# Two-block transformer forward on one core: first attention units and their normalizations reordered, GpSimd's bias in pieces, and the first two output tiles of a gated projection computed together

## The chip, the cores and the metric

One Trainium2 chip, one of its NeuronCores. The metric is the device time of one execution in microseconds, the median of several runs. TensorE is called PE here, its weight loads PEld, VectorE DVE, ScalarE ACT, GpSimd POOL, and SyncE, which only issues weight transfers, SP.

## What is computed

Two blocks in a row, each of two layers, on 256 tokens of width 1024 (the first block puts 16 extra tokens in front, so its tiles are 272 tokens wide). All matrices are float32. Two pieces matter for the change.

The first layer is an attention with eight heads in which each query attends to its 64 best keys only:

```python
q, k, v, qi, ki, wi = jnp.split(h @ w_in, A_SPLITS, axis=-1)
score = jnp.einsum('bqh,bqhs->bqs', wib, jax.nn.relu(s))      # s = qi . ki
_, idx = lax.top_k(score, k_top)
logits = jnp.einsum('bqgrd,bqkgd->bqgrk', qg, ksel) * scale + bias
p = jax.nn.softmax(logits, axis=-1)
o = jnp.einsum('bqgrk,bqkgd->bqgrd', p, vsel)
```

The first layer of the second block is a gated mixer:

```python
z = jax.nn.gelu(hn @ w_in, approximate=False)
u, v = jnp.split(z, 2, axis=-1)
v = layernorm(v, ln_g, ln_b)
sv = jnp.einsum('gij,bnjgc->bnigc', ws, vb) + b_s.T[None, None, :, :, None]
return (u * sv.reshape(B, S, GATE_DIM)) @ w_out
```

## The kernel before

Everything is held transposed, with the model's width on the partitions and tokens in the free dimension. The program is a list of stages (`STAGES`); in each, PE makes output tiles of 128 rows from 128x1024 blocks of weights. SP loads a block into one of four slots of `w_raw`; ACT writes its rounded part to `w_hi`, DVE the rest to `w_lo` (function `prep`, always three blocks ahead), and PE makes the product from two or three passes with them (`mm2`, `mm3`). A block's slot is free for the next when PE has counted `block_done`. Output tiles rotate through four PSUM banks, `stream`; `misc` are the other four. Each engine runs its own instructions strictly in order, and semaphores join the engines; the order of the work is written out by hand for each engine.

**First attention (stage "in", then `attention(att_a, ...)`).** There are 16 units (a head and a block of queries), eight of block A with 144 keys, then eight of block B with 272. For unit u, PE makes `logits` (L721, and L727 which adds the mask `keep` of the chosen keys), DVE adds the bias and takes the maximum (`score_a`, L2502), ACT takes the exponential (L1474), DVE multiplies by the inverse sum (`softmax_norm`: L2209, L2218), PE transposes (`turn_probs`, L749), ACT copies (L1484), and PE multiplies with the values (`outputs`, L762). Logits go alternately to `misc[0]` and `stream[2]`. On PE, `logits(0)` is followed by `after_first` (sums of squares of the last head, L711), `meta_logits` (the 16 extra tokens, L796) and `keep_warm(stream[2], 16)`, 16 products whose result nobody reads (L734). Then come `logits(1)` and the loop of the units: in turn u, `logits(u + 2)`, `turn_probs(u)`, `outputs(u - 1)`.

The choice of the 64 keys is a generator on DVE, `selection` (L2360, L2361: eight maxima and their replacement; L2364 writes the mask). It is advanced two steps in each of the last turns of stage "in" and for its last two steps at unit 0 in `rest_of_selection`, together with `query_sums` (L2384), on which POOL waits. POOL then computes factors (L1964, L1967) and four blocks of bias, `masked_bias` (L1979): block A, heads 0 to 3; block B, heads 0 to 3; then the same for heads 4 to 7 (`half == 1`). A unit's score waits for its block of bias.

**Gated mixer (stages "gv", "gu", "gout").** "gv" makes the v half, DVE normalizes it (L2701). "gu" makes 16 tiles of the u half; after tile g, PE does `spatial(g - 1)` (L1214), four small products into `misc[c % 2]`, which for c of 2 and more waits until DVE has read the result of c - 2 (`sv_read`, given by L2721). DVE turns it into a product (`gated(c)`: L2718, L2721, L2728), ACT rounds it (L1773), and POOL makes the low part (L2054), which counts `gp_lo`. "gout" multiplies with `w_out`: eight output tiles of two weight blocks each, 16 steps k of two passes (L619, L620), and step k of the first tile waits for `gp_lo` at k + 1. DVE adds each tile to `h` (L2140, L2143) and writes the low part of the next input (L2153, `low`); in this stage DVE runs a hardware loop of two turns of four tiles, PE four tiles written out and then one turn.

Of the kernel before, what the change touches and what calls it, by code (L numbers as in the profile page):

```python
# [20 lines left out]
ALU = mybir.AluOpType  # L21
# [3 lines left out]
P = 128  # L25
D = 1024
DT = D // P
META = 16
# [10 lines left out]
GT = GATE // P  # L39
# [6 lines left out]
R = 4  # L46
LR = 3
# [40 lines left out]
ST = {s.name: s for s in STAGES}  # L88
# [64 lines left out]
def build(nc, x, meta, table, w_in_a, w_o_a, w_kv_b, w_q_b, w_o_b, w_up, w_down, a_w_in, a_w_s,  # L153
          a_b_s, a_w_out, b_w_q_a, b_w_q_b, b_w_o, kv_w_a, kv_w_b, mlp_w1, mlp_w2, positions,
          vecs, lams, consts, onehot, out):
    with ExitStack() as ctx:
# [11 lines left out]
        wide_h, wide_l = split_w[:, 0, :], split_w[:, 1, :]  # L168
# [8 lines left out]
        ones = sb("ones", [P, P])  # L177
# [426 lines left out]
        def _(pe):  # L604
# [126 lines left out]
            def keep_warm(dst, n):  # L731

                for _ in range(n):
                    pe.matmul(dst[:, 0:T], xh[:, 0, 0:P], xh[:, 1, :], start=True, stop=True)  # L734
# [30 lines left out]
            def attention(att, q_of, v_of, after_first=None):  # L765
                n = len(att.units)
                own_meta = att.name != "c"
                logits(att, q_of, 0)
                if own_meta:
                    after_first()  # L770
                    meta_logits(att, q_of)
                    keep_warm(stream[2], 16)
                logits(att, q_of, 1)
                for u in range(n + 1):
                    if u + 2 < n:
                        logits(att, q_of, u + 2)
                    if u < n:
                        turn_probs(att, u)
                    if u == 8 and own_meta:
                        meta_turn(att)  # L780
                    if u == 11 and own_meta:
                        meta_outputs(att, v_of)
                    if u >= 1:
                        v = u - 1
                        if v >= 4 and v % 2 == 0:
                            pe.wait_ge(att.oh, att.ob + v // 2 - 1)
                            pe.wait_ge(att.ol, att.ob + v // 2 - 1)
                        outputs(att, v_of, v, PV_BANK[v // 2 % 2][:, P * (v % 2):P * (v % 2 + 1)])
# [133 lines left out]
            def up(name, t0, first=None):  # L922
# [31 lines left out]
                        product(s, i, g, **src)  # L954
                sweep(pe, s, group, peel=True)

            def down(name, t0, nk, stride, sem_, base):
                s = ST[name]

                def ready(k):  # L960
                    pe.wait_ge(sem_, base + k + 1)
                skip = stride - (T - t0)
                hid = lambda buf: lambda k: buf[:, k * stride + skip:(k + 1) * stride]
                both = None
                if name in HALVES:
                    both = lambda k: split_w[:, :, k * stride + skip:(k + 1) * stride]
                sweep(pe, s, lambda s, i, g: product(s, i, g, hid(wide_h), hid(wide_l), t0,
                                                     ready, nk, both), peel=True)

            simple("wo_a", lambda s: from_heads(att_a))  # L970
            up("up0", 0, CONV_IN[0])
# [247 lines left out]
            pe.wait_ge(S["tile_read"], s.t0)  # L1219
            for g in range(16):  # L1220
                product(s, None, g, **from_x(s, META))
                if g >= 1:
                    spatial(g - 1)
            spatial(15)
            down("gout", META, GT, 256, gp_lo, 0)
            up("mlp0", META)
            down("mlpd0", META, F2T, 256, mlp["lo"], 0)
# [666 lines left out]
        def _(pool):  # L1894
# [75 lines left out]
            def masked_bias(qt, half):  # L1970

                q, hi = TT[qt], TOK[qt][1]
                o = P if qt == "A" else 0
                dst = bias_a[qt][:, 4 * half:4 * half + 4, :]
                g = fq_a[:, 12 * half + q:12 * half + q + 10:3].unsqueeze(2)
                pool.wait_ge(roots_ready, 1 if half == 0 else 2 if qt == "A" else 3)
                pool.wait_ge(S["skew_loaded"], SKEW_IN)
                pool.wait_ge(skew_masked, 1)
                pool.tensor_tensor(dst, sk[:, 4 * half:4 * half + 4, o:o + hi],  # L1979
                                   g.to_broadcast([P, 4, hi]), ALU.mult).then_inc(bias_ready, 1)  # L1980

            pair_half = neg_half[:, 0:12].rearrange("p (m x) -> p m x", m=2)

# [88 lines left out]
        def _(dve):  # L2072
# [62 lines left out]
            def residual_stage(name, t0, straight=False, beside={}):  # L2135
# [23 lines left out]
                def group(s, i, g):  # L2159
                    for b in range(s.bpg - 1):  # L2160
                        prep(s, i, g * s.bpg + b)
                    add(s, i, g)
                    between = s.bpg == 1 and g % 4 != 3
                    if between:
                        prep(s, i, g)
                    low(s, i, g)
                    if not between:
                        prep(s, i, (g + 1) * s.bpg - 1)
                    if g in beside:
                        beside[g]()  # L2170
# [41 lines left out]
            def softmax_norm(att, v):  # L2212

                hh, qt = att.units[v]
                lo, hi = att.keys(qt)
                k = inverse_sums(att, v)
                p0 = lg[:, v % LR, 0, lo:hi]
                dve.tensor_scalar(p0, p0, ri[:, k:k + 1], None, ALU.mult).then_inc(att.p, 1)  # L2218

            def softmax_mix(att, v):  # L2220

# [262 lines left out]
            def rest_of_selection(u):  # L2484

                if u == 0:
                    dve.wait_ge(a_ssq, 10)
                    query_sums(att_a, 1)
                if u < 7:
                    next(selection, None)  # L2490
                if u == 0:
                    next(selection, None)
                if u == 16:
                    dve.wait_ge(att_a.mo0, att_a.meta + 1)
# [244 lines left out]
            stage("gu", gu_after)  # L2739
            gated(14)  # L2740
            gated(15)
            residual_stage("gout", META)

            def angles():

# [256 lines left out]
```

## Time and profile before

| | us |
|---|---|
| median of 3 runs | 1305.34 (1304.49 to 1305.48) |
| the profiled execution, its own time | 1305.53 |
| its span, first to last instruction | 1303.7 |
| around the span | 1.8 |
| PE busy | 1281.2 (98%) |
| DVE busy | 979.8 (75%) |
| ACT busy | 669.0 (51%) |
| POOL busy | 493.8 (38%) |
| mean granted clock of TensorE | 0.998 |

Busy times of PE are modelled ends of pipelined products, so that neighbours overlap; the start of a product against the start of the one before it tells more than its length. A number in square brackets behind a row of the timeline is the idle time of that engine just before the instruction, with the instruction that ended it.

### The profile page before, as it was taken

To read this page: it belongs to the slowest core of one execution; us is meant where nothing else is said; L and a number is where in the kernel's file an instruction comes from. 1 tells how busy PE (TensorE), PEld (TensorE's weight loads), DVE (VectorE), ACT (ScalarE), POOL (GpSimd) and SP (SyncE) were. 2 spreads that over 40 slices of the span, in tenths; PEclk is the share of its full clock that TensorE was granted. 3 is DMA by queue.
4 is the path that set the end of the run, shared out by engine and by line. 5 is a ranking of instruction groups with operands and counts; after the bars stand their busy time and mean duration, and the time that the engine had idled before them with its cause. 6 is when DMAs were issued, how large, how long until landed. Compare 5 with 4: busy or idle time off the path is not lost.

```text
span 1303.7 us, 26999 instructions
## 1 busy us (share of the span) xinstructions
PE 1281.2 (98%) x8914; PEld 1182.5 (91%) x8914; DVE 979.8 (75%) x1564; ACT 669.0 (51%) x1103; POOL 493.8 (38%) x454
## 2 busy tenths in 40 slices
PE   8999999999999999999999999999999999999998
PEld 7999999999999989999888898888888987888887
DVE  5686899975666668999765687799866866999553
ACT  5445555554455555666545455355444565455442
POOL 1042455541212216555311032299611001799222
PEclk9999999999999999999999999999999999999999
DMA  8631556566633316666567565666666642666762
GB/s 219 154 98 50 160 167 185 167 176 175 181 103 109 98 37 176 181 188 188 168 198 225 147 177 161 184 182 190 188 193 194 150 134 78 181 190 190 205 190 81
DMA packets 403204, 209.20 MB, mean 160 GB/s; under 512 B 20553, under 2 KB 397681, under 8 KB 403105
## 3 DMA queue, kind: packets, MB, share of 16 engines
q1 hardware_dynamic: 402016, 205.37, 55.0%
q0 software_dynamic: 784, 2.51, 0.8%
q8 instruction: 52, 0.85, 0.3%
q10 hardware_dynamic: 320, 0.21, 0.1%
q14 instruction: 32, 0.25, 0.1%
HBM read 206.98 MB, written 1.27 MB: 160 GB/s over the span
## 4 chain that ended last, share of the span: by engine, by line
PE 90%; DVE 6%; issue 2%; POOL 1%; ACT 1%; DMA 0%; DVEq 0%; POOLq 0%; ACTq 0%
PE bank L619 22%; PE bank L613 14%; PE bank L614 14%; PE bank L615 14%; PE bank L620 12%; DVE w_lo L2081 2%; PE bank L762 2%; PE bank L721 1%; PE bank L749 1%; PE bank L1184 1%; PE bank L1186 1%; PE bank L1185 1%; PE bank L1036 1%; PE bank L1023 1%; PE bank L691 1%
## 5 line engine op out<-in xcount | busy, mean ns | idle before, releaser
L2081 DVE TENSOR_TENSOR w_lo<-w_raw,w_hi 128x1024 fp32r<-128x1024 f32 x391 | 514.3, 1328 | 29.3 <-ACT w_hi L1441 28.4
L1441 ACT ACTIVATE w_hi<-w_raw 128x1024 fp32r<-128x1024 f32 x391 | 410.6, 1053 | 128.5 <-PE bank L620 66.0
L613 PE MATMUL bank<-split_x,w_lo 128*128 128x272 f32 (+2 forms) x1128 | 328.9, 292 | 0.2 <-issue 0.2
L615 PE MATMUL bank<-split_x,w_hi 128*128 128x272 f32 (+2 forms) x1128 | 322.5, 286 | 0.0
L614 PE MATMUL bank<-split_x,w_hi 128*128 128x272 f32 (+2 forms) x1128 | 322.4, 286 | 0.0
L619 PE MATMUL bank<-split_w,w_hi 128*128 128x512 f32 x880 | 307.7, 393 | 0.7 <-POOL split_w L1940 0.5
L620 PE MATMUL bank<-split_w,w_lo 128*128 128x256 f32 x880 | 246.6, 280 | 0.0
L613 PEld LDWEIGHTS bank<-split_x,w_lo 128*128 128x128 f32 x1128 | 212.2, 188 | 2.8 <-issue 0.6
L614 PEld LDWEIGHTS bank<-split_x,w_hi 128*128 128x128 f32 x1128 | 212.2, 188 | 0.3
L615 PEld LDWEIGHTS bank<-split_x,w_hi 128*128 128x128 f32 x1128 | 212.2, 188 | 0.3
L619 PEld LDWEIGHTS bank<-split_w,w_hi 128*128 128x128 f32 x880 | 164.9, 187 | 38.4 <-POOL split_w L1940 0.8
L619 PE MATMUL bank<-split_x,w_hi 128*128 128x512 f32 x512 | 179.5, 394 | 0.7 <-DVE split_x L2153 0.7
L620 PEld LDWEIGHTS bank<-split_w,w_lo 128*128 128x128 f32 x880 | 166.1, 189 | 0.0
L1915 POOL TENSOR_TENSOR sq_t<-h 128x256 f32<-128x256 f32 (+1 forms) x55 | 54.1, 984 | 250.6 <-DVE h L2143 250.1
L620 PE MATMUL bank<-split_x,w_lo 128*128 128x256 f32 x512 | 143.6, 281 | 0.0
L613 PE MATMUL bank<-split_w,w_lo 128*128 128x272 f32 (+1 forms) x444 | 130.5, 294 | 0.1
L615 PE MATMUL bank<-split_w,w_hi 128*128 128x272 f32 (+1 forms) x444 | 127.9, 288 | 0.0
L614 PE MATMUL bank<-split_w,w_hi 128*128 128x272 f32 (+1 forms) x444 | 127.4, 287 | 0.0
L619 PEld LDWEIGHTS bank<-split_x,w_hi 128*128 128x128 f32 x512 | 96.1, 188 | 22.7 <-DVE split_x L2153 1.0
L2529 DVE SCALAR_TENSOR_TENSOR scr<-scr,vec 128x256 f32<-128x256 f32 (+2 forms) x176 | 103.9, 600 | 12.7 <-ACT scr L1728 0.9
L1934 POOL TENSOR_TENSOR scr<-scr 128x272 f32<-128x272 f32 (+1 forms) x44 | 67.3, 1530 | 106.9 <-ACT scr L1735 85.0
L1728 ACT ACTIVATE scr<-scr,vec 128x272 f32<-128x272 f32 (+1 forms) x88 | 53.5, 608 | 101.0 <-DVE scr L2517 99.9
(295 smaller groups left out, 1855.9 us busy)
## 6 DMA issues: line engine op xcount, KB each, us to landing
w_raw<-in_mlp_w_dram SPq DMA_DIRECT2D x256, 256.0 KB, 3.2
w_raw<-in_w_up_dram SPq DMA_DIRECT2D x176, 256.0 KB, 3.3
w_raw<-in_w_down_dram SPq DMA_DIRECT2D x64, 256.0 KB, 3.4
w_raw<-in_a_w_in_dram SPq DMA_DIRECT2D x64, 256.0 KB, 3.5
w_raw<-in_w_in_a_dram SPq DMA_DIRECT2D x32, 256.0 KB, 4.1
w_raw<-in_w_kv_b_dram SPq DMA_DIRECT2D x32, 256.0 KB, 3.2
w_raw<-in_a_w_out_dram SPq DMA_DIRECT2D x32, 256.0 KB, 3.3
w_raw<-in_w_down_dram SPq DMA_DIRECT2D x32, 192.0 KB, 4.2
```

The costliest lines, as they stand in the source:

```text
L613: pe.matmul(dst, lo, mov_h, start=first, stop=False)
L614: pe.matmul(dst, hi, mov_l, start=False, stop=False)
L615: return pe.matmul(dst, hi, mov_h, start=False, stop=last)
L619: pe.matmul(dst.rearrange("p (s t) -> p s t", s=2), hi, both, start=first, stop=False)
L620: return pe.matmul(dst[:, 0:256], lo, mov_h, start=False, stop=last)
L762: ins = pe.matmul(dst, a, c, start=x_ == 0, stop=x_ == len(bls) - 1)
L1441: act.activation(w_hi[:, n % R, :], w_raw[:, n % R, :], ACT.Copy)\
L1728: act.activation(c_ring[:, g, c0:T], u_ring[:, g, c0:T], ACT.Identity, scale=vcol("conv_w", i, 4, o + 2 * UPT + g), bias=vcol("conv_b", i, ...
L1915: done(pool, pool.tensor_tensor(sq_t[:, t0:T], h[:, m, t0:T], h[:, m, t0:T], ALU.mult), "pool")
L1934: pool.tensor_tensor(gated, gated, c_ring[:, 2 * p, c0:T], ALU.mult)\
L2081: dve.tensor_tensor(w_lo[:, n % R, :], w_raw[:, n % R, :], w_hi[:, n % R, :].bitcast(F32), ALU.subtract)\
L2529: dve.scalar_tensor_tensor(c_, u_ring[:, q, lo - back:T - back], vcol("conv_w", i, 4, o + (CONV - 1 - back) * UPT + q), c_, ALU.mult, ALU. ...
```

## The change

In the first attention, PE makes `logits(1)` right behind `logits(0)`, with a wait for the reading of stage "in"'s tile 15 (it was the last to use `stream[3]`, and tile 14 the last to use `stream[2]`). The unread products go to `stream[3]` and are six in place of 16. DVE's last two steps of `selection` move from unit 0 to units 2 and 3. For units 0 to 5 DVE normalizes with an operation of three operands (the probabilities, the inverse sum, and a column of ones broadcast) in place of `tensor_scalar`. POOL computes both blocks of bias of heads 4 to 7 head by head, so eight operations in place of two.

In the gated mixer, `spatial(0)` moves behind tile 2 of "gu", directly ahead of `spatial(1)`. `spatial(15)` moves from ahead of "gout" to its first output tile, ahead of step k = 4. Output tiles 0 and 1 of "gout" are made in turns, in the new function `two_outputs`: steps 0 to 7 of tile 0, steps 0 to 7 of tile 1, steps 8 to 15 of tile 0, steps 8 to 15 of tile 1; the slot of tile 1's first block is counted free only with its second. DVE prepares both of the first tile's two blocks ahead of adding the tile, and its eight tiles are written out without a hardware loop.

```diff
                 logits(att, q_of, 0)
                 if own_meta:
+                    pe.wait_ge(S["tile_read"], ST["in"].t0 + 16)
+                    logits(att, q_of, 1)
                     after_first()
                     meta_logits(att, q_of)
-                    keep_warm(stream[2], 16)
-                logits(att, q_of, 1)
+                    keep_warm(stream[3], 6)
+                else:
+                    logits(att, q_of, 1)
...
+            def two_outputs(s, dst_of, mov_h, both, ready):
+
+                for g in range(2):
+                    bank_free(s, None, g)
+                for b in range(2):
+                    for g in range(2):
+                        j = 2 * g + b
+                        slot = (s.n0 + j) % R
+                        pe.wait_ge(S["lo_ready"], s.n0 + j + 1)
+                        for k in range(8 * b, 8 * b + 8):
+                            if g == 0 and k == 4:
+                                spatial(15)
+                            if g == 0:
+                                ready(k)
+                            w = slice((k - 8 * b) * P, (k - 8 * b + 1) * P)
+                            ins = mm2(dst_of(g), w_lo[:, slot, w], w_hi[:, slot, w], mov_h(k),
+                                      both(k), k == 0, k == GT - 1)
+                        if j != 2:
+                            ins.then_inc(S["block_done"], 2 if j == 3 else 1)
...
-                sweep(pe, s, lambda s, i, g: product(s, i, g, hid(wide_h), hid(wide_l), t0,
-                                                     ready, nk, both), peel=True)
+                def group(s, i, g):
+                    if name != "gout" or i is not None or g >= 2:
+                        product(s, i, g, hid(wide_h), hid(wide_l), t0, ready, nk, both)
+                    elif g == 0:
+                        two_outputs(s, lambda g: stream[(s.t0 + g) % R][:, :], hid(wide_h), both,
+                                    ready)
+                sweep(pe, s, group, peel=True)
...
                 product(s, None, g, **from_x(s, META))
-                if g >= 1:
+                if g == 2:
+                    spatial(0)
+                if g >= 2:
                     spatial(g - 1)
-            spatial(15)
             down("gout", META, GT, 256, gp_lo, 0)
...
-                pool.tensor_tensor(dst, sk[:, 4 * half:4 * half + 4, o:o + hi],
-                                   g.to_broadcast([P, 4, hi]), ALU.mult).then_inc(bias_ready, 1)
+                for hs in [slice(0, 4)] if half == 0 else [slice(e, e + 1) for e in range(4)]:
+                    ins = pool.tensor_tensor(dst[:, hs, :], sk[:, 4 * half:4 * half + 4, o:o + hi][:, hs, :],
+                                             g[:, hs, :].to_broadcast([P, hs.stop - hs.start, hi]),
+                                             ALU.mult)
+                ins.then_inc(bias_ready, 1)
...
+                    joined = s.name == "gout" and i is None and g == 0
+                    if joined:
+                        prep(s, i, g * s.bpg + 1)
                     add(s, i, g)
...
-                    if not between:
+                    if not between and not joined:
                         prep(s, i, (g + 1) * s.bpg - 1)
...
-                p0 = lg[:, v % LR, 0, lo:hi]
-                dve.tensor_scalar(p0, p0, ri[:, k:k + 1], None, ALU.mult).then_inc(att.p, 1)
+                probs = lg[:, v % LR, 0, lo:hi]
+                if att.name == "a" and v < 6:
+                    dve.scalar_tensor_tensor(probs, probs, ri[:, k:k + 1],
+                                             ones[:, 0:1].to_broadcast([P, hi - lo]), ALU.mult,
+                                             ALU.mult).then_inc(att.p, 1)
+                    return
+                dve.tensor_scalar(probs, probs, ri[:, k:k + 1], None, ALU.mult).then_inc(att.p, 1)
...
-                if u < 7:
-                    next(selection, None)
-                if u == 0:
+                if 2 <= u < 8:
                     next(selection, None)
...
-            residual_stage("gout", META)
+            residual_stage("gout", META, straight=True)
```

## Rows read from the trace of the kernel before

**Rows 1.** The page: busy time of each engine.

```profile
PE 1281.2 (98%) x8914; PEld 1182.5 (91%) x8914; DVE 979.8 (75%) x1564; ACT 669.0 (51%) x1103; POOL 493.8 (38%) x454
```

**Rows 2.** Chain that ended last, start of the attention: start us, us, what.

```profile
84.40 0.61 PE bank L711 x6
...
85.73 2.22 PE bank L734 x16
87.95 0.24 PE bank L721 x2
...
90.62 1.50 DVE scr L2218
...
92.16 0.44 PE bank L749 x2
```

**Rows 3.** Timeline of DVE and POOL in units 0 to 3.

```profile
84.67 0.37 DVE L2502 CUSTOM_DVE_ANT_0 scr<-bank,vbuf,small 128x144 f32<-128x144 f32 x1
...
85.44 0.43 DVE L2360 MAX8 small<-qk 128x8 f32<-128x272 f32 x1
...
86.45 0.30 DVE L2364 TENSOR_SCALAR split_w<-qk 128x272 fp32r<-128x272 f32 x1
...
86.89 1.15 POOL L1979 TENSOR_TENSOR vbuf<-skew,small 128x576 f32<-128x576 f32 x1
...
88.30 0.37 DVE L2502 CUSTOM_DVE_ANT_0 scr<-bank,vbuf,small 128x144 f32<-128x144 f32 x1 [1.54 <-PE bank L727]
...
88.78 0.30 DVE L2218 TENSOR_SCALAR scr<-scr,small 128x144 f32<-128x144 f32 x1
...
90.00 2.01 POOL L1979 TENSOR_TENSOR vbuf<-skew,small 128x1088 f32<-128x1088 f32 x1
...
90.62 1.48 DVE L2218 TENSOR_SCALAR scr<-scr,small 128x144 f32<-128x144 f32 x1
```

**Rows 4.** The same timeline earlier, where DVE and POOL meet.

```profile
77.20 1.96 DVE L2081 TENSOR_TENSOR w_lo<-w_raw,w_hi 128x1024 fp32r<-128x1024 f32 x1
78.04 2.99 POOL L1979 TENSOR_TENSOR vbuf<-skew,small 128x1088 f32<-128x1088 f32 x1
```

**Rows 5.** Line L2718 alone: duration ns min/median/max.

```profile
L2718 DVE SCALAR_TENSOR_TENSOR scr<-qk,vec x16: 341/344/830, 749.9 to 796.1; 128x128 f32<-128x128 f32 x16
```

**Rows 6.** Timeline at the start of "gu".

```profile
744.43 0.28 PE L614 MATMUL bank<-split_x,w_hi 128*128 128x256 f32 x1
744.54 0.28 PE L615 MATMUL bank<-split_x,w_hi 128*128 128x256 f32 x1
745.34 0.71 PE L1214 MATMUL bank<-qk,vbuf 128*128 128x128 f32 x4 [0.52 <-DVE vbuf L2701]
...
746.86 1.22 DVE L2081 TENSOR_TENSOR w_lo<-w_raw,w_hi 128x1024 fp32r<-128x1024 f32 x1
```

**Rows 7.** Timeline from "gu" to "gout".

```profile
792.92 0.71 PE L1214 MATMUL bank<-qk,vbuf 128*128 128x128 f32 x4 [0.85 <-DVE scr L2721]
...
797.98 0.40 PE L619 MATMUL bank<-split_w,w_hi 128*128 128x512 f32 x1
...
798.27 0.74 POOL L2054 TENSOR_TENSOR split_w<-scr,split_w 128x256 fp32r<-128x256 f32 x1 [0.81 <-ACT split_w L1773]
798.33 0.39 PE L619 MATMUL bank<-split_w,w_hi 128*128 128x512 f32 x1
...
799.06 0.50 PE L619 MATMUL bank<-split_w,w_hi 128*128 128x512 f32 x1 [0.23 <-POOL split_w L2054]
799.17 1.23 DVE L2081 TENSOR_TENSOR w_lo<-w_raw,w_hi 128x1024 fp32r<-128x1024 f32 x1 [1.43 <-ACT w_hi L1441]
```

**Rows 8.** Windows: us, busy PE, PEld, DVE, ACT, POOL, clock, DMA.

```profile
88.00:92.00 4.00, 2.55 (x20) 2.04 (x18) 3.33 (x12) 1.98 (x8) 3.84 (x4) 1.00 0.01 2
...
464.00:466.00 2.00, 1.24 (x10) 0.76 (x7) 1.86 (x6) 1.28 (x7) 0.68 (x1) 1.00 0.00 0
...
472.00:474.00 2.00, 2.00 (x11) 1.92 (x11) 0.03 (x1) 0.63 (x3) 0.00 (x0) 0.50 0.00 0
```

## The prediction

> **What bounds the kernel now.** I read the page first: PE is busy in 98% of the span, DVE in 75% [rows 1], and the chain of work that ended last runs on PE but for short pieces. Time is gained only where PE waits, so I looked up the idle times on PE at the places of the edits. There are three. In the first attention's start PE waits for normalized probabilities: the chain leaves PE for DVE's L2218 at 90.62 and comes back at 92.16 [rows 2]. At the start of "gu", `spatial(0)` waits for the layer normalization [rows 6]. Between "gu" and "gout", `spatial(15)` waits 0.85 us for DVE's reading of c = 13, and step 15 of the first tile waits for POOL's last low part [rows 7]. Everything behind each place runs off PE in the same order, so what PE wins there moves the end by as much, unless a new wait takes it back.
>
> **Attention, the order.** The reader is to see in [rows 3] that DVE does score 0 at 84.67, its sums and two selection steps until 86.75, and then idles 1.54 us until 88.30, for `logits(1)`. These start at 87.95 only, behind 2.22 us of unread products [rows 2]. The new order, step by step:
> - `logits(1)` starts at 84.40; DVE has it 0.35 later (87.95 to 88.30), at 84.75.
> - PE's sums of squares come 0.33 later (a unit's two products), end at 84.40 + 0.33 + 0.61 = 85.34. The meta logits took 85.73 - 85.01 = 0.72, and six unread products take 6 x 2.22/16 = 0.83: PE is at `logits(2)` at 86.89 and at `turn_probs(0)` at 87.2.
> - DVE: query sums from 85.34, 0.43 (85.01 to 85.44) to score 1 at 85.77; a score's start to its normalization's is 0.48 (88.30 to 88.78); so unit 0 is normalized from 86.25, ready at 86.6. PE doesn't wait at all.
> - Score 2 at 86.89 + 0.35 = 87.24, normalization 1 from 87.72, which meets POOL (below) and ends by 88.3. One selection step is 1.01 (85.44 to 86.45): score 3 at 89.2, normalization 2 from 89.7, ready at 90.05. `turn_probs(2)` starts at 90.1 in place of 92.16: 2.1 us earlier. The last selection step, 0.30, lies behind it and not ahead of it. The mask of block B is due at unit 8.
>
> **Attention, the three operands and the pieces.** The `tensor_scalar` of unit 2 took 1.48 in place of 0.30 and ended 0.09 behind POOL's bias of 2.01 [rows 3]: it was held until POOL was through. An operation with two tensors in SBUF is no better off by this trace. L2718 takes 0.344 and 0.830 at most, where it met POOL [rows 5]; L2081 began at 77.20, POOL's next operation at 78.04, and they took 1.96 and 2.99 against 1.22 and 2.01 alone [rows 3, 4, 6]: POOL ran up to 78.04, DVE got in between POOL's two operations, and the second then stood behind DVE. So whoever started first keeps the other out, and DVE gets its turn at the end of a POOL operation. The new form (probabilities and ones both in SBUF) still waits; the pieces shorten the wait. From 576 elements in 1.15 and 1088 in 2.01 an operation costs 0.18 plus 1.68 ns an element: a piece of block A is 0.42, of block B 0.64, and a block as a whole 0.54 longer. The Trainium skill has this as a rule (SBUF — State Buffer, Who interferes with whom): a Vector instruction with two SBUF inputs contends with a GpSimd instruction that reads SBUF, and the loser is blocked until the other is done. By that rule the three operands gain nothing here, the trace agrees (0.830 against 0.344), and were it wrong the sum would lack the collision term below.
>
> The new form was not run at this size; its nearest row is the score of 144 columns with two tensors, 0.37, against 0.30: 0.07 dearer, six times 0.4, of which only units on DVE's path count; above nothing and below 0.4, included in the times above.
> Bias A of heads 4 to 7 starts 0.33 later and takes 0.54 more, so it is ready at 86.89 + 0.33 + 1.15 + 0.54 = 88.9, at most 0.4 more for one DVE operation in between; unit 4's score comes at about 90.2. POOL's block B started 1.96 behind A's end, so now at about 91.1, and lasts until 94 to 94.5. Due at unit 12, it holds nobody; but the normalizations of units 4, 5 and 6 fall into it, each held from 0 to 0.64. PE's own work per unit hides part. I take 0.4 for the three (about the mean of 0.32 each, less half hidden); the bounds are 0 and 3 x 0.64 = 1.9. **Attention: 2.1 - 0.4 = 1.7 us gained, from 0.2 to 2.1.**
>
> **Start of "gu".** The last product of tile 1 starts at 744.54, its follower would start 0.12 later (744.43 to 744.54), at 744.66, and `spatial(0)` starts at 745.34 [rows 6]: 0.68 lost. Behind tile 2 (24 products, 24 x 0.118 = 2.8 us later) it finds its input. Does the new order run into the next thing? PE wants tile 3's weights at 744.66 + 2.83 + 2 x 0.45 = 748.4; they are ready at 746.86 + 1.22 = 748.08 [rows 6]. A margin of 0.3. **0.7 us gained, from 0.3 to 0.7.**
>
> **"gu" to "gout".** Before, PE stood 0.85 for `spatial(15)`. Now it does steps 0 to 3 of tile 0 meanwhile (four times 0.35, 797.98 to 798.33, makes 1.4 us), and comes to it after DVE's release. Step 15 of the first tile started at 799.06, where 798.33 + 0.35 = 798.68 was due: 0.38 lost [rows 7]. In the new order eight steps of tile 1 (2.8 us) stand ahead of it: due at about 800.7, POOL's part is there at 799.01. Taken off: 1.23; added, one more change between the two kinds of products, 0.1 (0 to 0.2). What could be late next are weights. Tile 1's second block is wanted at about 801.1 and ready at 799.17 + 1.23 = 800.4: margin 0.7. Tile 2's first (DVE's second preparation, now directly behind) at 801.6, wanted at 804. Tile 2's second needs only a slot that is free at 801.1. Tile 3's first needs the slot freed at 804; behind ACT's part and DVE's queue (adding tile 1, its low part, then 1.2 for the block) I estimate it at 808.6 for 809.6. These hold by 0.7 to 2.4. The DVE loop written out removes a loop step that is beside PE's work: nothing, and if its cover were gone 0.1. **1.1 us gained, from 0.4 (a late block) to 1.3.**
>
> **Sum.** 1.7 + 0.7 + 1.1 = 3.5 us. The profiled execution took 1305.53, 1.8 around its span of 1303.7, and stands 0.2 above the median; its time would be 1302.0, the median 1305.34 - 3.5 = 1301.8.
>
> **Rivals.**
> - Collisions decide. If each normalization of units 1 to 6 waits out a whole piece or more, the attention gains 0.2 to 0.8. For it: DVE holds [rows 3, 5], and more POOL operations give more chances to meet. Against: DVE gets in at the end of one [rows 4]. 0.5 + 0.7 + 1.1 = 2.3: 1303.0.
> - The clock falls in the attention, which has 1.4 us fewer unread products. It fell elsewhere: at 472 the granted clock was 0.50, 1.2 GHz in place of 2.4, after a stretch like 464 to 466, where PE was busy 1.24 of 2 us; from 88 to 92, 2.55 of 4, it stayed [rows 8]. In the new order PE waits less in that very stretch. A fall of some 3.4 us costs half, 1.7: 1303.5.
> - The joined tiles run into late weights and give back what they won, 1.1: 1302.9. Decides at the margins of 0.7 and 1.0 above.
> - The reordering doesn't do it: unit 0 or 1 waits on something else (the sums, the exponential), and only "gu" and "gout" win: 1303.5.
> - Slower: the clock stays down for all of the attention. From 87 to 99 at the lower level costs up to 6 us, against 3.5 won: 1307.8. It becomes slower from 7 us at the lower level on. Against it: PE is busier there than before, and before it kept its clock.
>
> **Chances.** My forecast 0.66, its own range 1300.9 to 1302.7 (the terms' likely ends); collisions 0.13; the falling clock 0.06; late weights 0.06; no effect in the attention 0.06; slower 0.03. The measurement tells 0.2%, 2.6 us, from no change. The forecast lies on the faster side nearly always (0.64), collisions and late weights in four of ten cases between them (0.07), the rest within: faster 0.71, same 0.26, slower 0.03. The range reaches to the collisions and the fall, 1300.8 to 1303.7.
>
> **What would show it.** L2502 of unit 1 without an idle time and some 2.5 us earlier; L749 of unit 2 about 2.1 us earlier; no L2218-like operation above 1 us, but the new ones of units 1, 4 and 5 above 0.4; no idle time ahead of the first L1214; none ahead of the last L1214 and of step 15; the granted clock 1.00 from 84 to 100. The prediction is wrong if PE's idle times come back as waits for `w_lo` in "gout", if unit 4 or 5 waits for its bias, or if the clock falls.

## The result and the profile after

The changed kernel took **1303.07 us** in the median of 20 runs (1300.08 to 1306.12), the kernel before 1305.34 in 20 runs beside it (1303.26 to 1307.72): the medians are 2.3 us apart. The recorded ratio is 0.9985, interval 0.9978 to 0.9991, which makes 1.2 to 2.9 us gained. The median is inside the range of 1300.8 to 1303.7, 1.3 above the forecast of 1301.8 and above the forecast's own range (1300.9 to 1302.7). It lies within 0.2% (2.6 us) of no change, where the prediction had put only 0.26 of its chances, against 0.71 for more than that.

The profiled execution of the changed kernel took 1300.44, with a span of 1298.6: 5.1 below the profiled execution of before, far more than the 2.3 of the medians. The page's first part of the changed kernel:

```profile
PE 1276.5 (98%) x8904; PEld 1178.4 (91%) x8904; DVE 981.2 (76%) x1564; ACT 669.3 (52%) x1103; POOL 496.7 (38%) x460
```

PE has ten products fewer (the unread ones) and POOL six operations more. To lay the two traces side by side I took the starts of DVE's blocks `w_lo` (the same 394 in every kernel, on L2081 before and L2114 after), whose pace is PE's. Three intervals hold nearly all of the difference: A from the block ahead of the first attention to the one behind it, B the last 31 us of the second attention, C from the first tiles of "gu" to the stage behind "gout".

| kernel, profiled execution | A | B | C |
|---|---|---|---|
| before | 37.14 | 30.70 | 94.88 |
| before again (e1) | 37.15 | 30.69 | 94.08 |
| changed | 35.67 | 29.59 | 92.01 |
| changed again (e2) | 35.66 | 32.27 | 91.95 |
| changed, a third time (e10) | 35.66 | 32.22 | 92.51 |

A, from such rows (timeline of DVE, kernel before, then the changed kernel; start us, us, what): 118.64 - 81.50 = 37.14, and 117.24 - 81.57 = 35.67.

```profile
81.50 1.23 DVE L2081 TENSOR_TENSOR w_lo<-w_raw,w_hi 128x1024 fp32r<-128x1024 f32 x1 [0.43 <-ACT w_hi L1441]
...
118.64 1.22 DVE L2081 TENSOR_TENSOR w_lo<-w_raw,w_hi 128x1024 fp32r<-128x1024 f32 x1
```

```profile
81.57 1.23 DVE L2114 TENSOR_TENSOR w_lo<-w_raw,w_hi 128x1024 fp32r<-128x1024 f32 x1 [0.43 <-ACT w_hi L1471]
...
117.24 1.22 DVE L2114 TENSOR_TENSOR w_lo<-w_raw,w_hi 128x1024 fp32r<-128x1024 f32 x1
```

A is the same to 0.01 in every execution of a kernel. B is not, and C has a part of 0.5 to 0.8 that comes and goes. The change touches nothing in B. The stretch ahead of A varies too: from the first block `w_lo` to the one at A's start it is 71.15 in the kernel before and 71.85 in e1, and 0.5 to 1.0 longer than 71.15 in five of the 14 profiles (e1, e2, e9, e10, e12), whichever the kernel.

**The attention after**, timelines of PE, DVE and POOL of the changed kernel, against [rows 2 to 4]; the whole trace is 0.08 later here than before:

```profile
86.94 0.41 PE L721 MATMUL bank<-qk 128*128 128x144 f32 x2
...
87.26 0.39 PE L749 MATMUL bank<-cst,scr 128*128 128x128 f32 x2
...
88.63 0.44 PE L749 MATMUL bank<-cst,scr 128*128 128x128 f32 x2 [0.68 <-DVE scr L2255]
...
90.42 0.44 PE L749 MATMUL bank<-cst,scr 128*128 128x128 f32 x2 [0.58 <-DVE scr L2255]
...
91.84 0.44 PE L749 MATMUL bank<-cst,scr 128*128 128x128 f32 x2 [0.23 <-DVE scr L2255]
```

```profile
85.87 0.36 DVE L2541 CUSTOM_DVE_ANT_0 scr<-bank,vbuf,small 128x144 f32<-128x144 f32 x1
...
86.35 0.37 DVE L2255 SCALAR_TENSOR_TENSOR scr<-scr,small,ones 128x144 f32<-128x144 f32 x1
87.46 0.37 DVE L2541 CUSTOM_DVE_ANT_0 scr<-bank,vbuf,small 128x144 f32<-128x144 f32 x1 [0.74 <-PE bank L727]
...
87.94 0.63 DVE L2255 SCALAR_TENSOR_TENSOR scr<-scr,small,ones 128x144 f32<-128x144 f32 x1
...
90.97 0.82 DVE L2255 SCALAR_TENSOR_TENSOR scr<-scr,small,ones 128x144 f32<-128x144 f32 x1
```

```profile
87.22 1.65 POOL L2010 TENSOR_TENSOR vbuf<-skew,small 128x144 f32<-128x144 f32 x4
...
90.98 2.67 POOL L2010 TENSOR_TENSOR vbuf<-skew,small 128x272 f32<-128x272 f32 x4
```

The reader is to see that `turn_probs(2)` starts at 90.42 where it was 92.16, that the two long normalizations (0.63 and 0.82, the others 0.37) meet POOL's pieces of bias (87.94 lies inside the row from 87.22; the row at 90.97 starts 0.01 ahead of POOL's at 90.98 and was held all the same), and that nothing is held as long as the 1.48 of before.

**"gu" and "gout" after**, timelines of PE and DVE, against [rows 6, 7]:

```profile
744.88 0.28 PE L615 MATMUL bank<-split_x,w_hi 128*128 128x256 f32 x1
745.00 1.05 PE L1243 MATMUL bank<-qk,vbuf 128*128 128x128 f32 x8
...
788.17 0.61 PE L1243 MATMUL bank<-qk,vbuf 128*128 128x128 f32 x4
788.54 0.47 PE L619 MATMUL bank<-split_w,w_hi 128*128 128x512 f32 x1
...
789.89 0.28 PE L620 MATMUL bank<-split_w,w_lo 128*128 128x256 f32 x1
790.01 0.60 PE L1243 MATMUL bank<-qk,vbuf 128*128 128x128 f32 x4
790.37 0.48 PE L619 MATMUL bank<-split_w,w_hi 128*128 128x512 f32 x1
...
805.37 0.39 PE L619 MATMUL bank<-split_w,w_hi 128*128 128x512 f32 x1
...
805.90 0.47 PE L619 MATMUL bank<-split_w,w_hi 128*128 128x512 f32 x1
```

```profile
803.58 1.08 DVE L2186 SCALAR_TENSOR_TENSOR split_x<-h,vec,split_x 128x272 fp32r<-128x272 f32 x1 [0.79 <-ACT split_x L1488]
804.59 2.34 DVE L2114 TENSOR_TENSOR w_lo<-w_raw,w_hi 128x1024 fp32r<-128x1024 f32 x2
```

`spatial(0)` and `spatial(1)` (one row of eight products at 745.00) and `spatial(15)` (790.01) start 0.12 behind the product ahead of them: no wait. One new loss is there: a step of 805.90 - 805.37 = 0.53 where 0.35 is usual, as the first block of tile 3 came late. DVE's low part ahead of it took 1.08 (0.50 four us earlier), beside an operation of POOL (803.62 to 804.36).

### The profile page after: what moved, and what is told of

Read it like the earlier page. It is cut to its first block, busy times and chain, and to the rows that moved or that the text cites. A ratio compares the mean times of both kernels' runs of the same rounds, so it can differ in the third digit from the quotient of the medians.

```text
span 1298.6 us, 26922 instructions
## 1 busy us (share of the span) xinstructions
PE 1276.5 (98%) x8904; PEld 1178.4 (91%) x8904; DVE 981.2 (76%) x1564; ACT 669.3 (52%) x1103; POOL 496.7 (38%) x460
## 4 chain that ended last, share of the span: by engine, by line
PE 90%; DVE 6%; issue 1%; POOL 1%; ACT 1%; DMA 0%; DVEq 0%; POOLq 0%; ACTq 0%
PE bank L619 23%; PE bank L613 15%; PE bank L615 14%; PE bank L614 14%; PE bank L620 12%; DVE w_lo L2114 1%; PE bank L762 1%; PE bank L721 1%; PE bank L1213 1%; PE bank L1215 1%; PE bank L1214 1%; PE bank L749 1%; PE bank L1065 1%; PE bank L1052 1%; PE bank L1243 1%
## 5 line engine op out<-in xcount | busy, mean ns | idle before, releaser
L2114 DVE TENSOR_TENSOR w_lo<-w_raw,w_hi 128x1024 fp32r<-128x1024 f32 x391 | 517.8, 1337 | 29.9 <-ACT w_hi L1471 28.9
```

The lines of the kernel that those rows point to most:

```text
L2114: dve.tensor_tensor(w_lo[:, n % R, :], w_raw[:, n % R, :], w_hi[:, n % R, :].bitcast(F32), ALU.subtract)\
```

## The experiments

Each was timed beside the kernel before, whose median was 1305.17 for e1 to e4, 1305.33 for e5 to e8 and 1305.34 for e9 to e12.

### e1 and e2: both kernels again

The kernel before and the changed one, nothing altered.

> The kernel before, unchanged, for its spread and for the granted clock of each of its runs. Theory 1 (the changed kernel gains 1.5 in the attention, 0.8 at the start of gu and 1.1 between gu and gout, and the clock falls as often as before): its runs' clocks spread like those of the changed kernel, from 0.994 to 0.998, and at one clock it is 3.4 us or more slower. Theory 2 (fewer unread products let the clock fall more often in the changed kernel, which takes back some 2 us of the median): its clocks lie higher, at 0.997 to 0.998 in most runs, and the time stays at 1305.3.

> The changed kernel, unchanged, beside the kernel before on one chip. Both theories: ratio 0.9975 to 0.999. Theory 2: again clocks of 0.994 to 0.998 with the time 1.3 us longer for each 0.001, and more than one level among its runs. The profile is wanted for the step time of gout: 0.347 us in the first profile of the changed kernel, 0.353 in the one of before. If it belongs to the kernel's order it is 0.347 again and 0.353 in the run of before; if it is chance, it varies.

e1: 1305.14, ratio 1.0 (0.999 to 1.0009). e2: 1303.22, ratio 0.998 (0.997 to 0.9991). So the gain of about 2 stands, and the 5.1 of the profiled execution doesn't: e2's own profile has B at 32.27 in place of 29.59. The windows of both profiles there, first the changed kernel's, then e2's (stretch, length, busy PE, PEld, DVE, ACT, POOL, granted clock, DMA):

```profile
464.00:466.00 2.00, 0.99 (x14) 0.95 (x15) 1.90 (x7) 1.27 (x5) 0.00 (x0) 1.00 0.00 0
466.00:468.00 2.00, 2.00 (x19) 1.85 (x18) 1.90 (x7) 1.92 (x8) 0.02 (x1) 1.00 0.00 0
...
472.00:474.00 2.00, 1.78 (x13) 1.59 (x14) 1.31 (x5) 1.43 (x5) 0.28 (x1) 1.00 0.00 0
```

```profile
466.00:468.00 2.00, 2.00 (x11) 2.00 (x10) 1.93 (x7) 1.68 (x8) 0.00 (x0) 0.50 0.00 0
468.00:470.00 2.00, 2.00 (x15) 1.75 (x14) 1.12 (x5) 1.07 (x5) 0.70 (x1) 0.76 0.00 0
470.00:472.00 2.00, 2.00 (x16) 1.69 (x16) 0.53 (x4) 1.18 (x4) 0.30 (x1) 1.00 0.00 0
472.00:474.00 2.00, 2.00 (x13) 1.83 (x13) 0.44 (x1) 0.93 (x4) 0.25 (x1) 0.60 0.00 0
474.00:476.00 2.00, 2.00 (x12) 2.00 (x11) 0.64 (x2) 0.45 (x2) 0.00 (x0) 0.55 0.00 0
```

The granted clock is the column of 1.00, 0.50 and so on. It stayed at 2.4 GHz through this stretch in one execution of the changed kernel and fell to 1.2 GHz twice in another; in the kernel before it fell once [rows 8]. B reads 29.59 without a fall (changed, e6, e12), 30.68 to 30.70 with one (before, e1, e3, e4, e5, e7, e8), 32.09 to 32.27 with two (e2, e10, e11): 1.1 us for one, 2.5 to 2.7 for two.

### e3, e4 and e8: the parts alone

e3 is the kernel before with all of the change's edits in the attention; e4 the kernel before with all of those in the gated mixer; e8 the kernel before with `spatial(0)` moved alone. The core of each, in this order:

```diff
+                    logits(att, q_of, 1)
                     after_first()
                     meta_logits(att, q_of)
-                    keep_warm(stream[2], 16)
+                    keep_warm(stream[3], 6)
```

```diff
+                    elif g == 0:
+                        two_outputs(s, lambda g: stream[(s.t0 + g) % R][:, :], hid(wide_h), both,
+                                    ready)
...
-            spatial(15)
             down("gout", META, GT, 256, gp_lo, 0)
```

```diff
                 product(s, None, g, **from_x(s, META))
-                if g >= 1:
+                if g == 2:
+                    spatial(0)
+                if g >= 2:
                     spatial(g - 1)
```

> The kernel before with the attention's edits alone. Theory 1: 1.5 us faster, ratio 0.9989. Theory 2: the clock falls more often, and the ratio is 1.000 or above, with clocks of 0.994 to 0.997 in many runs.

> The kernel before with the edits of gu and gout alone. Theory 1: 1.9 us faster, up to 2.7 if the faster steps of gout belong to the order: ratio 0.9980 to 0.9986. Theory 2: the same, and clocks as for the kernel before, so that this part alone gives more than the whole change.

> The kernel before with spatial(0) behind tile 2 and nothing else. The first wait, 0.68 to 0.78 us, goes: 1304.5, ratio 0.9994. Its profile is also one more look at gout in the old order: steps of 0.347 or 0.353 us, and whether they change at the stall ahead of step 15 of tile 0. If the step time belongs to the order, it is 0.353 behind the stall; in a new look at the kernel before it was 0.347, so it should be either.

| | us, median | ratio | A | B | C |
|---|---|---|---|---|---|
| e3, attention | 1304.37 | 0.9993 (0.9984 to 1.0002) | 35.66 | 30.68 | 94.89 |
| e4, mixer | 1303.02 | 0.9987 (0.9978 to 0.9996) | 37.14 | 30.69 | 92.00 |
| e8, `spatial(0)` | 1304.41 | 0.9994 (0.9985 to 1.0003) | 37.15 | 30.70 | 93.34 |

In the traces each part gives what it gives in the whole: the attention 37.14 - 35.66 = 1.48, `spatial(0)` 94.08 - 93.34 = 0.74 against e1, and the joined tiles 93.34 - 92.00 = 1.34. Their sum is 3.56. In the medians the mixer gives 2.15 and the attention only 0.8; e3's interval reaches from 2.1 faster to 0.3 slower, so it holds the 1.48 as well. e4 doesn't tell the joined tiles, the move of `spatial(15)` and the written-out DVE loop apart; no run has one of them alone.

### e5: 16 unread products again

The changed kernel, with 16 unread products in the first attention in place of 6.

```diff
-                    keep_warm(stream[3], 6)
+                    keep_warm(stream[3], 16)
```

> The changed kernel with 16 unread products in stream[3] in place of six. Theory 1 (the falls of the clock have nothing to do with the attention): logits(2) stands 10 x 0.139 = 1.4 us later behind them, so this is up to 1.0 us slower than the changed kernel, 1304.0, with mean clocks of 0.996 as before. Theory 2 (fewer unread products let the clock fall): the clocks go back to 0.998 in most runs as in the kernel before, and the time is 1302 to 1303, faster than the changed kernel or level with it.

1303.16, ratio 0.9982 (0.9974 to 0.9991). A is 36.87: only 0.27 below the kernel before, and 1.20 above the changed kernel. Yet the median is no higher than that of the changed kernel (1303.07, 1303.22 and 1303.13 in its three sets of runs): what ten products cost in A doesn't show in it, and e11 below takes that up.

### e6: the three operands undone

The changed kernel with `tensor_scalar` for the normalizations again.

```diff
-                if att.name == "a" and v < 6:
-                    dve.scalar_tensor_tensor(probs, probs, ri[:, k:k + 1],
-                                             ones[:, 0:1].to_broadcast([P, hi - lo]), ALU.mult,
-                                             ALU.mult).then_inc(att.p, 1)
-                    return
```

> The changed kernel with tensor_scalar for units 0 to 5 again. By the rows of before an operation with two tensors in SBUF is held as well as this one: no change beyond 0.4 us (0.07 less for each of six), 1303.1. In the profile L2218's successor takes 0.30 where it is free and 0.5 to 0.8 where it meets a piece of the bias. The rival, that the three operands escape POOL: normalizations above 0.8 us appear, and the time is 0.5 us or more longer.

1302.97, ratio 0.9984 (0.9972 to 0.9995); A is 35.65, against 35.67 and 35.66. The three-operand form wins nothing. Its cheapest row is 0.37 where `tensor_scalar` takes 0.30; the longest are alike. By form, L2255 of the changed kernel and then L2254 of e6, in the first units (busy us, mean ns | idle before):

```profile
L2255 DVE SCALAR_TENSOR_TENSOR scr<-scr,small,ones 128x144 f32<-128x144 f32 x6 | 2.9, 488 | 0.2
```

```profile
L2254 DVE TENSOR_SCALAR scr<-scr,small 128x144 f32<-128x144 f32 x8 | 3.5, 442 | 0.3
```

### e7: the bias in whole blocks again

The changed kernel with two operations in place of the eight.

```diff
-                for hs in [slice(0, 4)] if half == 0 else [slice(e, e + 1) for e in range(4)]:
-                    ins = pool.tensor_tensor(dst[:, hs, :], sk[:, 4 * half:4 * half + 4, o:o + hi][:, hs, :],
...
+                pool.tensor_tensor(dst, sk[:, 4 * half:4 * half + 4, o:o + hi],
+                                   g.to_broadcast([P, 4, hi]), ALU.mult).then_inc(bias_ready, 1)
```

> The changed kernel with the two blocks of bias of heads 4 to 7 as one operation each. If the lock goes by operations, unit 1's normalization is held until block A is through (some 1.1 us in place of 0.63) and unit 3's or 4's until block B is through (1.5 to 2.0), so the attention wins 0.5 to 1.5 us less: 1303.7 to 1304.6. If the pieces have no effect: 1303.1 and the same chain.

1303.31, ratio 0.9987 (0.9978 to 0.9996). The median can't tell; A can: 36.52, so the pieces are worth 0.85 us. The rows are plain (e7, timelines of DVE, POOL and PE):

```profile
90.61 1.70 DVE L2252 SCALAR_TENSOR_TENSOR scr<-scr,small,ones 128x144 f32<-128x144 f32 x1
```

```profile
90.14 2.01 POOL L2009 TENSOR_TENSOR vbuf<-skew,small 128x1088 f32<-128x1088 f32 x1
```

```profile
92.36 0.44 PE L749 MATMUL bank<-cst,scr 128*128 128x128 f32 x2 [1.11 <-DVE scr L2252]
```

Unit 3's normalization began at 90.61, inside POOL's one long operation (90.14 to 92.15), was held to its end, and PE waited 1.11 for it. With pieces the same normalization took 0.82 and PE waited 0.23.

### e10 and e11: what ten unread products do in both attentions

e10 is the changed kernel a third time. e11 is the kernel before with one line altered:

```diff
-                    keep_warm(stream[2], 16)
+                    keep_warm(stream[2], 6)
```

> The changed kernel again, beside the other three on one chip. 1303.2, with clocks of 0.996 or lower in about half of its runs (32 of 55 so far among it and the two variants with six unread products and both parts of the change).

> The kernel before with six in place of 16 unread products in the first attention, nothing else. DVE waits for logits(1), which come 1.4 us earlier: score 1 at 86.9 in place of 88.3. Theory 1: unit 0 is ready 1.4 us earlier; POOL's block B of the bias stays where it is, at 90.0 to 92.0, and holds unit 2's or a later unit's normalization less, so 0.5 to 1.4 us faster, clocks as before (none at 0.996). Theory 2, that fewer unread products in the first attention make the falls: clocks of 0.996 and lower in half of the runs, and no gain in the median.

e10: 1303.13, ratio 0.998 (0.9971 to 0.9989). e11: 1305.61, ratio 0.9997 (0.9988 to 1.0006), although A is 36.05. So six unread products alone, in the old order, win 1.09 in A, and it doesn't show in the median. Where it went can be read in e11's profile, B = 32.09, two falls (windows):

```profile
466.00:468.00 2.00, 2.00 (x10) 2.00 (x11) 1.97 (x5) 1.53 (x8) 0.00 (x0) 0.50 0.00 0
468.00:470.00 2.00, 2.00 (x16) 1.75 (x14) 1.33 (x7) 1.36 (x5) 0.70 (x1) 0.80 0.00 0
470.00:472.00 2.00, 2.00 (x17) 1.69 (x17) 0.47 (x3) 1.18 (x4) 0.23 (x1) 1.00 0.00 0
472.00:474.00 2.00, 2.00 (x13) 1.92 (x12) 0.50 (x1) 0.66 (x3) 0.32 (x1) 0.56 0.00 0
```

Every run gives its mean granted clock. In the profiles 0.997 to 0.999 stands for one fall or none in B, 0.996 for two, 0.994 for one of 10 us (e9). The mean isn't a clean count of falls in B, since every profile has one more at its end, behind PE's last product, which costs PE nothing but takes 0.001 to 0.002 off the mean. For runs without a profile the falls are inferred from this number. I counted the runs at 0.996 or below, with the mean time in each group:

| kernel | unread products, first attention | runs at 0.996 or below | mean us there | mean us at 0.998 |
|---|---|---|---|---|
| before | 16 | 7 of 96 | 1308.48 | 1305.15 |
| e1, e4, e5, e8 | 16 | 6 of 45 | | |
| e11 | 6 | 6 of 11 | 1306.21 | 1304.01 |
| changed, first 20 runs | 6 | 13 of 20 | 1304.17 | 1301.40 |
| e2, e10 | 6 | 13 of 22 | | 1301.60 (e10) |
| e6, e7 | 6 | 13 of 24 | | 1301.35 (e6) |
| e3 | 6 | 1 of 11 | 1307.50 | 1303.37 |

At a mean clock of 0.998 (which holds runs with one fall and some without) the changed kernel is 1305.15 - 1301.40 = 3.75 us faster, about the sum of the terms. That rests on four runs, from 1300.08 to 1302.78; e2 against the kernel before on its own chip gives the same, 1305.46 - 1301.68 = 3.8 at 0.997 and 1304.13 - 1300.28 = 3.9 at 0.999 (three and two runs of e2). The changed kernel's median is only 2.3 lower because more than half of its runs have, by their mean clock, a second or a long fall, and where a profile shows one it lies in the second attention, 370 us behind the edit. Six in place of 16 unread products in the first attention go with it: e11 differs from the kernel before by nothing else, on the same chip, and had 6 of 11 such runs against 2 of 28; and e5, the changed kernel with 16, had 1 of 11. What became frequent is a mean of 0.996, in the profiles two falls: 33 of 88 runs with six, 2 of 141 with 16. At 0.995 or below there are 13 of 88 and 11 of 141. e3 speaks against the simple form of that: it has six as well, and only 1 of 11.

### e9 and e12: unread products in the second attention

In both, PE makes six more unread products in the last units of the second attention, where it otherwise waits 0.86 us for DVE. The longer wait of 1.06 just behind stays as it was (timelines of PE, the changed kernel and then e9):

```profile
462.35 0.52 PE L1013 MATMUL bank<-cst,acc 128*128 128x128 f32 x3 [0.86 <-DVE split_w L2640]
...
465.01 0.35 PE L810 MATMUL bank<-cst,sq_t 16*16 16x16 f32 x8 [1.06 <-DVE sq_t L2345]
```

```profile
463.03 0.52 PE L1013 MATMUL bank<-cst,acc 128*128 128x128 f32 x3
...
465.70 0.36 PE L810 MATMUL bank<-cst,sq_t 16*16 16x16 f32 x8 [1.07 <-DVE sq_t L2346]
```

The six cost the path nothing there: between these two rows lie 2.66 us in the changed kernel and 2.67 in e9, and `logits_b(15)` ahead of them starts 1.95 and 1.94 before the first.

```diff
             turn_probs(att_b, 12)
             logits_b(15)
+            keep_warm(stream[3], 6)
```

e9 is the changed kernel with that; e12 has 16 unread products in the first attention as well:

```diff
-                    keep_warm(stream[3], 6)
+                    keep_warm(stream[3], 16)
```

> The changed kernel with six more unread products in the second attention's last units, behind logits_b(15), where PE idles 0.9 us. In all ten profiles so far the clock fell only there, between 465 and 473 us, once or twice or not at all. If the falls there spread the changed kernel's runs (1300 to 1306), the granted clock rises to 0.998 or 0.999 in most runs, and the median comes to 1301.5 (4 us below the kernel before). If unread products have no hold on the falls: clocks of 0.994 to 0.998 as for the changed kernel, 1303.2.

> The changed kernel with 16 unread products in the first attention and six more in the second. Theory 1: 0.5 to 1.0 us slower than with six and six, the work of the unread products in the first attention, 1302.3. Theory 2: fewer falls than with six and six, and level with it or faster.

| | us, median | runs | ratio | runs at 0.996 or below |
|---|---|---|---|---|
| e9 | 1301.40 (1300.80 to 1305.21) | 6 | 0.9967 (0.9954 to 0.9979) | 1 of 6 |
| e12 | 1302.42 (1301.56 to 1302.99) | 11 | 0.9978 (0.9969 to 0.9987) | 0 of 11 |
| e10, beside them | 1303.13 (1300.07 to 1305.98) | 11 | 0.998 (0.9971 to 0.9989) | 7 of 11 |

e12 has no run at 0.996 or below and a spread of 1.4 us where e10 has 5.9; it pays with A = 36.87. What its six products in the second attention add to that isn't shown, as e5, without them, had only 1 of 11. e9 keeps A = 35.66 and gives the lowest median, 3.9 below the kernel before, as much as the whole sum of the terms. Its one profiled run is the one with the long fall (B = 33.85):

```profile
466.00:468.00 2.00, 2.00 (x13) 2.00 (x11) 1.93 (x5) 1.55 (x8) 0.00 (x0) 0.59 0.00 0
468.00:470.00 2.00, 2.00 (x10) 1.75 (x9) 1.56 (x7) 1.39 (x5) 0.70 (x1) 0.50 0.00 0
...
474.00:476.00 2.00, 2.00 (x12) 1.92 (x11) 0.22 (x1) 0.37 (x2) 0.03 (x1) 0.50 0.00 0
```

So six products there do not exclude a fall. With six runs, and an interval that overlaps that of e10, e9 has the lowest median and isn't proven better.

## Why the prediction was right or wrong

| term | predicted, us | measured in the traces | by |
|---|---|---|---|
| attention | 1.7 (0.2 to 2.1) | 1.47 | A: 37.14 - 35.67, and e3 |
| start of "gu" | 0.7 (0.3 to 0.7) | 0.74 | C: e1 against e8 |
| "gu" to "gout" | 1.1 (0.4 to 1.3) | 1.34 | C: e8 against e4 |
| sum | 3.5 | 3.55 | |
| median | 1301.8 | 1303.07 | |

**The sum** agrees to 0.05, in part by luck: the attention gave 0.23 less and "gu" to "gout" 0.24 more than forecast. **The range** held in part by luck as well: from 1302.7 up it was there for two rivals, collisions and a fall in the attention, and neither happened as put.

**Attention, the order: right in its steps.** `turn_probs(0)` was forecast for 87.2 and came at 87.26 without a wait; `turn_probs(2)` 2.1 earlier, and came 1.74 earlier in a trace that starts 0.08 later, so 1.82. The missing 0.3 is unit 1: its normalization took 0.63 and PE waited 0.68 for it, where the prediction let it end by 88.3. **The collisions** were to give back 0.4 of it, and 1.82 - 1.47 = 0.35 was given back; PE's row at 91.84 shows 0.23 of that as a wait for unit 3's normalization. The pieces were priced right: 1.65 for the four of block A (0.42 each forecast, so 1.69) and 2.67 for those of block B, at 90.98 (91.1 forecast). Which units would meet them was forecast wrongly: the sum took 0.4 for units 4, 5 and 6, and units 1 and 3 it was, so the agreement of 0.35 with 0.4 is luck. "Whoever started first keeps the other out" fails for starts this close: unit 3's row starts 0.01 ahead of POOL's and was held. The rival "collisions decide" is refuted as it was put.

**The three operands** were forecast to win nothing, and e6 shows it (35.65 against 35.67). POOL's bias holds both forms: `tensor_scalar` took 0.74 at 90.58 in e6, the new form 0.82 at 90.97. The rule cited from the Trainium skill (SBUF — State Buffer, Who interferes with whom) agrees: in e7 the instruction with two inputs in SBUF was blocked until the other was done, 1.70 in place of 0.37. What makes the edit pay are the pieces, 0.85 (e7).

**What the prediction didn't separate** is how much of the attention's 1.47 comes from the new order. It put the gain down to the order, but six unread products in place of 16 alone give 1.09, in the old order (e11); the order, the pieces and the new form add 36.05 - 35.67 = 0.38 to that, and give 0.27 with 16 (e5). So the two parts nearly add up (1.36), and three quarters of the gain is ten unread products fewer, the same edit that goes with more falls of the clock. Without the pieces, the new order with six gives 37.14 - 36.52 = 0.62 (e7), less than the old order with six. The old order with six and the pieces was not run, so what the new order wins by itself stays open.

**Start of "gu"** came out as worked out: `spatial(0)` without a wait, and the margin of 0.3 for tile 3 held. **"gu" to "gout"**: both stalls are gone, and the term was too small. It took off the recorded idle time of 0.85 ahead of `spatial(15)`, which leaves out that PE's rows overlap. By starts, `spatial(14)` needs 788.54 - 788.17 = 0.37 in the changed kernel, and before it was 1.46 from its start to that of `spatial(15)` at 792.92, so 1.09 was lost. The row of `spatial(14)` before:

```profile
791.46 0.61 PE L1214 MATMUL bank<-qk,vbuf 128*128 128x128 f32 x4
```

One block was late, tile 3's first, for which 1.0 of margin had been estimated: PE lost about 0.2 at 805.37, as DVE's low part took 1.08 beside POOL. The rival "late weights" is right in kind; it put 1.1 on it, five times what the block cost.

**The step that failed is "everything behind each place runs off PE in the same order, so what PE wins there moves the end by as much, unless a new wait takes it back".** The one new wait cost 0.2. But the time of the second attention isn't fixed: its granted clock falls not at all, once, twice or for 10 us (B from 29.59 to 33.85), and the changed kernel has the costlier cases in more than half of its runs, judged by their mean clock. The sum of 3.5 was made for a profile with one fall. At equal clock it holds (3.75), and the median kept 2.3 of it. The rival "the clock falls in the attention, which has 1.4 us fewer unread products", 0.06 at 1303.5, is what happened in kind, and wrong in place and price: it put 1.7 on a fall, and one cost 1.1. That its 1303.5 is near the median is chance. From 84 to 100 the clock stayed at 1.00 in every profile, for instance here in the changed kernel and in e11, and it fell between 465 and 477.

```profile
88.00:92.00 4.00, 2.55 (x19) 2.19 (x20) 3.86 (x16) 2.40 (x10) 3.84 (x7) 1.00 0.01 2
```

```profile
88.00:92.00 4.00, 3.08 (x23) 2.62 (x23) 3.37 (x13) 2.63 (x12) 3.84 (x4) 1.00 0.01 2
```

**What stays open.** That six in place of 16 unread products in the first attention make the second fall more frequent is shown by e11 and e5 in counts, by no mechanism. PE's work just ahead doesn't explain it: the changed kernel, which had no fall, and e10, which had two, have the same rows there, 1.14 us apart, with the same waits of 0.86 and 1.06 (timeline of PE, e10):

```profile
466.15 0.35 PE L810 MATMUL bank<-cst,sq_t 16*16 16x16 f32 x8 [1.06 <-DVE sq_t L2345]
```

The profiles do show two places. In e2, e9, e10 and e11 the first or long fall begins within 0.7 us of the end of this wait; in the seven profiles with a single short fall it begins 4.8 to 5.6 us behind it. So the same work meets a fall at one place, at the other or at neither. e3, with six unread products and 1 of 11, fits no rule I have: its code up to the second attention, and through it, is that of the changed kernel. Against e2's 6 of 11 on the same chip so uneven a split comes by chance about once in 16 times, so chance isn't excluded. Whether the falls follow the number of products, the moment at which the second attention is reached or something else was not settled. The expectation of e9 says that the clock fell only there; that leaves out the fall at the end of every profile.

## What to carry to other kernels

Before adding up gains from one profile, look at the granted clock of all runs: a kernel whose TensorE sits at the edge of a fall has medians that move by as much as such edits win, and a profiled execution can be 2.6 us off its own median. Price unread products by what they do everywhere; where PE waits anyway they cost the path nothing (e9), though it isn't shown that they prevent falls there. And when a short VectorE operation on the path meets a long GpSimd one, cutting the GpSimd one into pieces can pay (0.85 here), even though the pieces cost more in all (1.65 for 1.15 and 2.67 for 2.01); another form of the VectorE operation didn't.

## What the runs showed of the hardware

- A fall of the granted clock in the second attention cost 1.1 us, two cost 2.5 to 2.7, and one of about 10 us cost 33.85 - 29.59 = 4.3.
- The steps of "gout" have two speeds. In the kernel before they started 0.353 us apart, in the same kernel again (e1) 0.347, for more than a hundred steps, at a granted clock of 1.00 in both. The 20 steps between these rows (timeline of PE, the kernel before and then e1) took 831.68 - 824.61 = 7.07 and 831.35 - 824.42 = 6.93:

```profile
824.61 0.40 PE L619 MATMUL bank<-split_w,w_hi 128*128 128x512 f32 x1
...
831.68 0.40 PE L619 MATMUL bank<-split_w,w_hi 128*128 128x512 f32 x1
```

```profile
824.42 0.39 PE L619 MATMUL bank<-split_w,w_hi 128*128 128x512 f32 x1
...
831.35 0.39 PE L619 MATMUL bank<-split_w,w_hi 128*128 128x512 f32 x1
```

  That is 0.8 of interval C (94.88 and 94.08) for one and the same kernel. The profiled execution of the changed kernel had the faster speed, so its 5.1 is the sum of 3.55, the absent fall (1.1) and this 0.8, less some 0.3 lost in small pieces elsewhere. In these profiles the speed changes only where PE stalled. It changed at the wait ahead of step 15 of tile 0 in the kernel before (0.347 ahead of it, 0.353 behind) and in e1 (the other way), and in the changed order only at tile 3's late block, behind which four of nine profiles (e6, e7, e10, e12) went on at 0.353. Why a stall changes it is open.
